# Expert stage of a transformer block: 32 by 32 turns on VectorE, two buffers for fetched rows, gate and up in four column tiles each

## The chip, the cores and the metric

One core of a Trainium2 chip runs the whole program. The metric is the device time of one execution in microseconds (us). The engines are TensorE (PE in the profile, with PEld for its weight loads), VectorE (DVE), ScalarE (ACT), GpSimd (POOL) and SyncE (SP), which issues most transfers. A profiled execution gives the trace that is read here.

## The reference, cut to what matters

The block attends and mixes (left out here), then sends each of 2048 tokens to two of 32 experts:

```
def hierarchical_moe(h, w_rg, w_re, w_g, w_u, w_d):
    ...
    eid = (group_idx[:, None] * EXPERTS_PER_GROUP + top_i.astype(jnp.int32)).reshape(-1)
    ...
    def expert_block(args):
        xb, e = args
        return (jax.nn.silu(xb @ w_g[e]) * (xb @ w_u[e])) @ w_d[e]
    ...
    y = jnp.sum(out[slot_dest].reshape(n_tok, TOP_K, D) * gates[..., None].astype(h.dtype), axis=1)
```

D_MODEL is 1024, D_EXPERT 512, everything is float32. An expert has three matrices of 2 MB each.

## The kernel before

The program runs in stages: projections, attention, time mixing, then the three stages that the change touches.

- `mix_out_and_route` (L1726): for each of 16 tiles of 128 tokens, the output projection, the second norm (h2, written to DRAM at L1781) and the router. `by_chunk` (L1720) reorders the channels within each row of h2, so that a block of 128 columns of h2 holds every fourth channel of a half. The router's weights w_r and the experts' weights are loaded in the same order (L1684, L1792, L1793).
- `place_slots` (L1984): the tables that say for each block of 32 rows which token rows to fetch (`from_all`), where to add the result (`to_all`) and the gate of each row (`gate_all`). Each of the 32 experts has at least two blocks of 32 rows; with these inputs there are 144 blocks.
- `run_experts` (L2132): the 144 blocks. All five engines run loops over the blocks and wait for each other by semaphores that count blocks.

In `run_experts` a block is 32 token rows. Every row is stored as four quarters of 256 channels on four partitions, so that a fetched block `xg` is 128 partitions by 256. POOL fetches it with an indirect DMA (`gather`, L2214), and adds a finished block to the output with another (L2225, 128 partitions by 256 as well). There is one buffer xg. TensorE turns xg with two 128 by 128 transposes (`turn`, L2249), ScalarE and VectorE copy one half each to xT. `gate_up` (L2255) works in four column tiles of 32: two take gate's halves of 256 columns, two take up's, all into one tile gu_ps, in 8 steps over the channels. ScalarE makes silu of the gate half, VectorE multiplies it with the row's gate and the up half to h (L2371). TensorE turns h by two transposes (`turn_h`, L2262), ScalarE copies it to hT, and `down` (L2270) multiplies it with wd in four column tiles of 256 columns and 4 steps. ScalarE and VectorE copy one half of y each (L2329, L2360).

TensorE's order in a block b (`one_block`, L2274) is: first half of gate_up(b), turn_h (block b-1), second half of gate_up(b), turn(b+1), down(b-1). Its code is a loop over three experts (L2305), and for each expert a first block and an inner loop over the others (L2289), so the loop over three experts holds six block bodies. POOL's order in a block (`one_block`, L2217) is: wait for the turn of xg, fetch, wait for y, add. VectorE's semaphore wait for the landing of an earlier add (`stored`) stands ahead of its copy of y. SP loads the weights of expert e+3 when expert e's last down is done (`refill`, L2195), twelve transfers of 512 KB.

A float32 matmul of the code stands in the trace as two MATMUL records, each with its LDWEIGHTS record; a transpose stands as one. So a block has 64 records of gate_up, 32 of down and 4 of transposes, and as many weight loads.

Of the kernel before, what the change touches and what calls it, by code (L numbers as in the profile page):

```python
# [20 lines left out]
ALU = mybir.AluOpType  # L21
# [1630 lines left out]
class ExpertWeights:  # L1652
# [20 lines left out]
    def load(self, sp, turn, s, part=None):  # L1673

        w_g, w_u, w_d = self.dram
        e = turn % N_GROUPS * PER_GROUP + turn // N_GROUPS
        for x, (to, src) in enumerate(((self.wg, w_g), (self.wu, w_u))):
            if part in (None, x):  # L1680
                rows = src[0, bass.ds(e, 1), :, :].rearrange("o (h p k) f -> p (o h) k f", h=2, p=P)
                for h in range(2):
                    for ks in (slice(0, 2), slice(2, 4)):
                        sp.dma_start(to[s][:, 4 * h + ks.start:4 * h + ks.stop, :], rows[:, h, ks, :]).then_inc(self.gu_loaded[s], 16)  # L1684
        if part in (None, 2):
            rows = w_d[0, bass.ds(e, 1), :, :].rearrange("o (f p) d -> p (o f) d", p=P)
            for f in range(FF // P):
                sp.dma_start(self.wd[s][:, f, :], rows[:, f, :]).then_inc(self.d_loaded[s], 16)
# [31 lines left out]
def by_chunk(row):  # L1720


    return row.rearrange("t (p k) -> t k p", p=P)


def mix_out_and_route(nc, program, E_all, ranks, gates, totals, x, norm2_gain, w_rg, w_re, experts, mix, ps, x1_dram, h2_dram):  # L1726


    with ExitStack() as ctx:
# [42 lines left out]
        with nc.Block() as block:  # L1772
            @block.sync
            def _(sp):
# [15 lines left out]
                for h in range(2):  # L1790
                    ks, rows = slice(4 * h, 4 * h + 4), slice(512 * h, 512 * h + 512)
                    sp.dma_start(w_r[:, ks, 0:N_GROUPS], w_rg[0, rows, :].rearrange("(p k) c -> p k c", p=P)).then_inc(weights, 16)  # L1792
                    sp.dma_start(w_r[:, ks, N_GROUPS:NL], w_re[0, rows, :].rearrange("(p k) c -> p k c", p=P)).then_inc(weights, 16)  # L1793
# [44 lines left out]
            def _(pe):  # L1838
# [13 lines left out]
                def one_tile(t, s, n, first, last):  # L1852
# [12 lines left out]
                    if first:  # L1865
                        pe.wait_ge(weights, 64)
# [37 lines left out]
            def _(dve):  # L1904
# [8 lines left out]
                def norm(t, s, n):  # L1913
# [9 lines left out]
                    for half in range(2):  # L1923
                        cols = slice(512 * half, 512 * half + 512)
                        done = dve.scalar_tensor_tensor(h2[:, s, cols].rearrange("t (k p) -> t k p", p=P), by_chunk(x_t[:, s, cols]), rstd[:, :],
                                                        by_chunk(gain[:, cols]), ALU.mult, ALU.mult)
# [57 lines left out]
def place_slots(nc, program, E_all, ranks, totals, gates, n_blocks, first_block, n_pairs, from_all, to_all, gate_all):  # L1984
# [5 lines left out]
    with ExitStack() as ctx:  # L1990
        sb, pb, sem = makers(nc, ctx, program)
        QUARTERS = [slice(q * ROWS, (q + 1) * ROWS) for q in range(4)]
        LO, HI = QUARTERS[0], slice(2 * ROWS, 4 * ROWS)
# [14 lines left out]
        spread = sb("spread", [ROWS, 4, ROWS])  # L2008
# [4 lines left out]
        token_ps, gate_ps, to_ps = pb("token_ps", [P, 512]), pb("gate_ps", [P, 512]), pb("to_ps", [P, 512])  # L2013
# [4 lines left out]
        with nc.Block() as block:  # L2018
            @block.gpsimd
            def _(pool):  # L2020
# [7 lines left out]
                pool.affine_select(out=spread[:, :, :], in_=spread[:, :, :], compare_op=ALU.not_equal, fill=1.0, base=0,  # L2028
                                   pattern=[[0, 4], [-1, ROWS]], channel_multiplier=1)
# [12 lines left out]
            def _(pe):  # L2042
                for part in range(PARTS):
                    pe.wait_ge(rows_ready, part * 2 + 2)
                    pe.wait_ge(gates_ready, part + 1)
                    for col in range(part * EACH, (part + 1) * EACH):
                        first, last = col == 0, col == 2 * NT - 1
                        pe.matmul(token_ps[LO, 0:TABLE], row_token[:, col, :], in_block[:, col, :], start=first, stop=last)
                        for q in (2, 3):
                            done = pe.matmul(gate_ps[QUARTERS[q], 0:TABLE], row_gate[:, col, :], in_block[:, col, :], start=first, stop=last)  # L2050
                done.then_inc(tabled, 1)
                pe.wait_ge(to_ready, 1)
                pe.matmul(to_ps[:, 0:TABLE], spread[:, :, :].rearrange("t q r -> t (q r)"), to_f[:, :], start=True, stop=True).then_inc(spread_done, 1)

            @block.vector
            def _(dve):
# [59 lines left out]
                dve.tensor_copy(gate_all[HI, :], gate_ps[HI, 0:TABLE])  # L2116
# [3 lines left out]
                dve.tensor_copy(to_row[:, :], to_ps[:, 0:TABLE])  # L2120
                dve.drain()
# [10 lines left out]
def run_experts(nc, program, n_blocks, first_block, n_pairs, from_all, to_all, gate_all, experts, h2_dram, out):  # L2132
# [6 lines left out]

    with ExitStack() as ctx:  # L2140
# [3 lines left out]
        LO, HI = slice(0, 2 * ROWS), slice(2 * ROWS, 4 * ROWS)  # L2144
# [5 lines left out]
        xg = sb("xg", [P, 2, P])  # L2150
        xT = sb("xT", [P, 2, 4, ROWS])
# [292 lines left out]
```

## Time and profile before

| | us |
|---|---|
| median of 3 runs | 3070.25 (3064.46 to 3083.59) |
| the profiled execution, its own time | 3088.86 |
| its span, first to last instruction | 3086.9 |
| the expert stage in it | about 2067 to 3080 |

Durations come from that one profiled execution. The mean granted clock of TensorE over its span is 0.973 of 2.4 GHz.

### The profile page before, as it was taken

What the parts mean: (1) busy time and instruction counts of PE and PEld (TensorE: products, weight loads), DVE (VectorE), ACT (ScalarE), POOL (GpSimd) and SP (SyncE); (2) the same over time, 40 slices, a digit from 0 to 9 for tenths busy, and PEclk for the clock granted to TensorE, in tenths of its full rate; (3) what the DMA queues carried; (4) which work ended last, traced back from release to release, by engine and by line L of the source; (5) the groups of instructions that cost most, each with busy time, mean ns of one, the idle gap of its engine ahead of it and who ended that gap; (6) DMA issues with size and microseconds to landing.
All of it is one profiled execution on the core that took longest, in us unless ns stands there. A gap on an engine that the chain in (4) does not pass through costs nothing. (4 is left out here: it accounts for less than half of the span.)

```text
span 3086.9 us, 87281 instructions
## 1 busy us (share of the span) xinstructions
PE 2812.0 (91%) x36552; PEld 1653.7 (54%) x36553; DVE 1277.1 (41%) x2547; ACT 975.2 (32%) x2057; POOL 808.5 (26%) x818
## 2 busy tenths in 40 slices
PE   8999999999999996888888899959888899898988
PEld 4444444444666665777777455534444444444444
DVE  2333221114887885667666244442222222222222
ACT  1211100003666665555554234311211112121211
POOL 0000300000110104666655000023333333333333
PEclk9999999999999998999999999969999999999999
DMA  3212131112022020111110255326777766777682
GB/s 127 68 51 68 46 112 54 61 61 91 8 69 66 10 91 22 38 42 43 39 52 25 70 204 203 116 103 201 236 236 239 236 218 208 260 242 253 202 280 42
DMA packets 208454, 370.01 MB, mean 120 GB/s; under 512 B 35057, under 2 KB 134897, under 8 KB 205554
## 3 DMA queue, kind: packets, MB, share of 16 engines
q1 hardware_dynamic: 180450, 328.72, 30.9%
q0 software_dynamic: 27792, 38.16, 6.3%
q8 instruction: 170, 2.79, 0.4%
q14 instruction: 42, 0.34, 0.0%
HBM read 296.30 MB, written 70.52 MB: 119 GB/s over the span
## 5 line engine op out<-in xcount | busy, mean ns | idle before, releaser
L2255 PE MATMUL gu_ps<-wg_,xT 128*32 128x256 f32 x3168 | 383.1, 384 | 7.0 <-issue 4.2
L2255 PE MATMUL gu_ps<-wu_,xT 128*32 128x256 f32 x3168 | 383.0, 384 | 0.0
L712 DVE TENSOR_TENSOR_SCAN h_all<-h_all 128x512 f32<-128x512 f32 (+3 forms) x320 | 345.8, 1130 | 69.0 <-ACT h_all L664 42.9
L344 PE MATMUL ps<-low,high 128*128 128x512 f32 x768 | 337.2, 596 | 2.4 <-issue 2.4
L2225 POOL DMA_INDIRECT out<-y,put x144 | 228.8, 1589 | 302.2 <-DVE y L2360 292.3
L2270 PE MATMUL y_ps<-wd_,hT 128*32 128x256 f32 x4608 | 297.2, 401 | 0.0
L2353 DVE COPY xT<-xT_ps 128x128 f32<-128x128 f32 x145 | 42.4, 292 | 534.7 <-PE xT_ps L2249 534.7
L2255 PEld LDWEIGHTS gu_ps<-wg_,xT 128*32 128x32 f32 x3168 | 180.4, 111 | 140.0 <-issue 22.3
L1714 PE MATMUL ps<-high 128*128 128x512 f32 x512 | 231.4, 602 | 8.5 <-DMA high<-mixT 8.1
L344 PEld LDWEIGHTS ps<-low,high 128*128 128x128 f32 x768 | 144.4, 191 | 173.0 <-issue 173.0
L2214 POOL DMA_INDIRECT xg<-h,take x147 | 145.7, 991 | 343.8 <-DVE take L2363 320.6
L690 POOL TENSOR_SCALAR_AFFINE_SELECT h_all<-h_all 128x256 f32<-128x256 f32 x64 | 39.8, 622 | 703.5 <-ACT h_all L664 703.3
L2270 PEld LDWEIGHTS y_ps<-wd_,hT 128*32 128x32 f32 x4608 | 140.6, 114 | 108.1 <-issue 39.4
L444 PE MATMUL ps<-h_all,w_first 128*128 128x512 f32 x448 | 193.6, 592 | 0.0
L664 ACT ACTIVATE h_all<-ps 128x1024 f32<-128x1024 f32 (+3 forms) x160 | 143.7, 899 | 151.6 <-PE ps L617 151.5
L2255 PE MATMUL gu_ps<-high,xT 128*32 128x256 f32 x2880 | 176.4, 386 | 0.0
L2255 PEld LDWEIGHTS gu_ps<-wu_,xT 128*32 128x32 f32 x3168 | 176.0, 111 | 0.0
L628 PEld LDWEIGHTS ps<-ident,h_all 128*128 128x128 f32 x1088 | 116.0, 141 | 106.9 <-DVE h_all L712 76.6
L444 PE MATMUL ps<-h_all,low 128*128 128x512 f32 x384 | 165.8, 592 | 0.0
L628 PE MATMUL ps<-ident,h_all 128*128 128x128 f32 x1088 | 154.8, 281 | 4.6 <-DVE h_all L712 4.1
L1714 PEld LDWEIGHTS ps<-high 128*128 128x128 f32 x512 | 95.1, 192 | 114.7 <-issue 114.0
L2249 PE MATMUL xT_ps<-ident,xg 128*128 128x128 f32 x292 | 64.1, 302 | 101.0 <-DMA xg<-h,take 101.0
(320 smaller groups left out, 4579.3 us busy)
## 6 DMA issues: line engine op xcount, KB each, us to landing
wd_<-in_w_exp_down SPq DMA_DIRECT2D x128, 512.0 KB
wg_<-in_w_exp_gate SPq DMA_DIRECT2D x88, 512.0 KB
wu_<-in_w_exp_up SPq DMA_DIRECT2D x88, 512.0 KB
high<-in_w_exp_gate SPq DMA_DIRECT2D x40, 512.0 KB
high<-in_w_exp_up SPq DMA_DIRECT2D x40, 512.0 KB
pT<-low SPq DMA_DIRECT2D x13, 1024.0 KB, 3.9
rkv<-pT SPq DMA_DIRECT2D x96, 128.0 KB, 2.5
high<-in_x SPq DMA_DIRECT2D x16, 512.0 KB, 4.0
```

Of the source, the lines that this page charges most:

```text
L344: done = pe.matmul(qkv_ps[:, part, :], hT[:, s, k, :], w_sb[:, k, part * SBW:(part + 1) * SBW], start=(k == 0), stop=(k == KT - 1))
L444: last = pe.matmul(p_ps[:, s, g, :], w[s][:, k, :], h_all[:, k, g * GT:(g + 1) * GT], start=(k == 0), stop=(k == KT - 1))
L628: last = pe.transpose(prodT_ps[h][:, b * P:(b + 1) * P], prod[:, n % KEPT, h, b * P:(b + 1) * P], ident[:, :])
L664: act.activation(keep[:, n % KEPT, :, 0:w], z_ps[n % 2][:, :, 0:w], ACT.Sigmoid, scale=-SCALE).then_inc(kept, 1)
L712: dve.tensor_tensor_scan(prod[:, n % KEPT, h, 0:w][:, ::-1], rows, rows, so_far, ALU.mult, ALU.bypass).then_inc(scanned, 1)
L1714: done = pe.matmul(self.ps[:, s, half, :], self.rows[:, s, k, :], self.w[:, k, half * 512:(half + 1) * 512], start=(k == 0), stop=(k == KT ...
L2214: pool.indirect_dma_start(out=xg[:, :, :].rearrange("t a b -> t (a b)"), out_offset=None, in_=h2_quarters[:, :], in_offset=bass.IndirectOf ...
L2225: pool.indirect_dma_start(out=out_quarters[:, :], out_offset=bass.IndirectOffsetOnAxis(ap=put[j][:, 0:1], axis=0), in_=y[j][:, :], in_offs ...
L2249: last = pe.transpose(xT_ps[j][:, 0:P], xg[:, j, :], ident[:, :])
L2255: last = pe.matmul(gu_ps[QUARTERS[q], 0:256], xT[:, k % 2, k // 2, :], w[s][:, k, half * 256:(half + 1) * 256], start=(k == 0), stop=(k == ...
L2270: last = pe.matmul(y_ps[QUARTERS[q], 0:256], hT[:, f % 2, f // 2, :], wd[s][:, f, q * 256:(q + 1) * 256], start=(f == 0), stop=(f == FT - 1))
L2353: dve.tensor_copy(xT[:, 1, :, :], xT_ps[1][:, 0:P].rearrange("p (q t) -> p q t", q=4)).then_inc(xT_ready, 1)
```

## The change

- The experts' turns move from TensorE to VectorE, whose transpose turns each 32 by 32 piece by itself (128 by 256 for the rows, 128 by 128 for h). The layouts of h2, of w_r and of the experts' weights are reordered to fit. The PSUM tiles of the turns, ident and both copies behind each turn are gone.
- xg becomes two buffers with a semaphore each. POOL fetches block b+4 into the buffer of b once h of block b+1 is done.
- Gate and up get a PSUM tile each and four column tiles of 128 columns each: 32 matmuls of the code for gate, then 32 for up, where there were 32 of 256 columns for both.
- sil, h and gate are 128 partitions wide instead of 64. ScalarE copies all of y alone. VectorE writes `put`, the row numbers for the add, at the end of its block, and waits for `stored` there.
- place_slots makes one copy of the gates and spreads it to four with one more matmul; w_r is loaded in 16 transfers instead of 4; the norm's last step is 4 instructions of 256 columns instead of 2 of 512.

```diff
-                rows = src[0, bass.ds(e, 1), :, :].rearrange("o (h p k) f -> p (o h) k f", h=2, p=P)
-                for h in range(2):
-                    for ks in (slice(0, 2), slice(2, 4)):
-                        sp.dma_start(to[s][:, 4 * h + ks.start:4 * h + ks.stop, :], rows[:, h, ks, :]).then_inc(self.gu_loaded[s], 16)
+                rows = src[0, bass.ds(e, 1), :, :].rearrange("o (p k) f -> p (o k) f", p=P)
+                for k in range(0, KT, 2):
+                    sp.dma_start(to[s][:, k:k + 2, :], rows[:, k:k + 2, :]).then_inc(self.gu_loaded[s], 16)
...
+                for j in range(4):
+                    for cols, src in ((slice(0, N_GROUPS), w_rg), (slice(N_GROUPS, NL), w_re)):
+                        rows = src[0].rearrange("(q p h j) c -> j h p q c", q=4, p=32, h=2, j=4)
+                        for h in range(2):
+                            sp.dma_start(w_r[32 * j:32 * j + 32, h::2, cols], rows[j, h]).then_inc(weights, 16)
...
-                def one_block(b, j, i, first):
-                    pool.wait_ge(turned, b + 3)
-                    pool.sem_inc(on_pool, 1)
-                    pool.wait_ge(rows_known, b + 4)
-                    pool.sem_inc(on_pool, 1)
-                    gather(1 - j)
-                    pool.wait_ge(y_copied, b * 2 + CREDIT + 2)
+                def add(b, j):
+                    pool.wait_ge(rows_known, b + 3)
                     pool.sem_inc(on_pool, 1)
+                    pool.wait_ge(y_copied, b + CREDIT + 1)
+                    pool.sem_inc(on_pool, 1)
                     pool.indirect_dma_start(out=out_quarters[:, :], out_offset=bass.IndirectOffsetOnAxis(ap=put[j][:, 0:1], axis=0),
                                             in_=y[j][:, :], in_offset=None, compute_op=ALU.add).then_inc(stored[j], 16)
+                def one_block(b, j, i, first):
+                    pool.wait_ge(h_ready, b + 3)
+                    pool.sem_inc(on_pool, 1)
+                    gather(j)
+                    add(b, j)
...
+                def project(to_ps, w, done):
+                    for k in range(KT):
+                        for q in range(4):
+                            last = pe.matmul(to_ps[QUARTERS[q], 0:P], xT[:, k * ROWS:(k + 1) * ROWS], w[:, k, q * P:(q + 1) * P],
                                              start=(k == 0), stop=(k == KT - 1))
+                    last.then_inc(done, 1)
+
+                def gate_up(b, s):
+                    pe.wait_ge(h_ready, b + 1)
+                    project(gate_ps, wg[s], gate_done)
+                    project(up_ps, wu[s], up_done)
...
                 def rest_of_expert(e, start, s):
                     with pe.Fori(1, count_of(pe, e)) as n:
-                        one_block(start + n, start + n - 1, s, s)
+                        gate_up(start + n, s)
+                        down(start + n - 1, s)
...
+                def turn_rows(j, i):
+                    dve.wait_ge(gathered[j], i * 16 + 16)
+                    dve.transpose(xT[:, :], xg[j][:, :])
+
+                def number_rows(b, j, i):
                     if not isinstance(i, int) or i > 0:
                         dve.wait_ge(stored[j], i * 16)
+                    dve.tensor_copy(put[j][:, :], to_all[:, bass.ds(b, 1)]).then_inc(rows_known, 1)
...
                 def one_block(b, j, i, first):
-                    dve.tensor_copy(gate[j][HI, :], gate_all[HI, bass.ds(b, 1)])
+                    dve.tensor_copy(gate[j][:, :], gate_all[:, bass.ds(b, 1)])
                     dve.drain()
-                    copy_xT(b + 1)
+                    dve.wait_ge(up_done, b + 1)
+                    turn_rows(1 - j, i + j)
                     next_rows(1 - j, b + 3)
                     dve.wait_ge(silu_ready, b + 1)
-                    dve.scalar_tensor_tensor(h[HI, :], sil[HI, :], gate[j][HI, :], gu_ps[HI, 0:256],
-                                             ALU.mult, ALU.mult).then_inc(h_ready, 1)
+                    dve.scalar_tensor_tensor(h[:, :], sil[:, :], gate[j][:, :], up_ps[:, 0:P], ALU.mult, ALU.mult).then_inc(h_ready, 1)
+                    dve.drain()
                     if not first:
-                        copy_y(b - 1, 1 - j, i - 1 + j)
+                        dve.wait_ge(y_done, b)
+                    dve.transpose(hT[:, :], h[:, :]).then_inc(hT_ready, 1)
+                    number_rows(b, j, i)
```

## Rows read from the trace of the kernel before

**Rows 1.** Busy time by stretch: busy us of each engine (records), clock, DMA.
```profile
1950.00:2000.00 50.00, 50.00 (x178) 26.89 (x177) 21.98 (x85) 20.40 (x30) 0.00 (x0) 1.00 0.30 111
2400.00:2600.00 200.00, 180.94 (x2845) 97.19 (x2838) 47.59 (x171) 39.24 (x128) 72.99 (x58) 0.97 0.70 220
1214.00:1708.00 494.00, 415.08 (x14597) 369.63 (x14598) 338.03 (x587) 254.08 (x517) 297.06 (x308) 0.99 0.14 39
```

**Rows 2.** Waits of the expert stage, then SP's own: us in total, times, longest.
```profile
PE xT_ps L2249 <- DMA xg<-h,take: 101.0, 47, 12.3
...
SPq L1684 <- PE y_ps L2270: 694.1, 29, 42.5
```

**Rows 3.** Chain of waits, pieces in the expert stage: start, us, what.
```profile
2112.10 7.14 DMA xg<-h,take
2149.03 5.56 DMA xg<-h,take
2356.69 8.29 DMA xg<-h,take
3070.35 2.77 DMA xg<-h,take
```

**Rows 4.** Timeline of TensorE in undisturbed blocks: start, us, records.
```profile
2079.86 0.44 PE L2249 MATMUL xT_ps<-ident,xg 128*128 128x128 f32 x2
2085.95 0.44 PE L2249 MATMUL xT_ps<-ident,xg 128*128 128x128 f32 x2
...
2403.55 0.39 PE L2255 MATMUL gu_ps<-wg_,xT 128*32 128x256 f32 x2
2403.77 0.39 PE L2255 MATMUL gu_ps<-wg_,xT 128*32 128x256 f32 x2
2405.39 0.33 PE L2262 MATMUL hT_ps<-ident,h 64*128 64x64 f32 x2
```

**Rows 5.** TensorE's first wait, a later one, and the clock behind it.
```profile
2067.18 0.66 PE L2249 MATMUL xT_ps<-ident,xg 128*128 128x128 f32 x2 [12.30 <-DMA xg<-h,take]
...
2119.38 0.66 PE L2249 MATMUL xT_ps<-ident,xg 128*128 128x128 f32 x2 [2.50 <-DMA xg<-h,take]
...
2119.40:2122.80 3.40, 3.40 (x30) 1.62 (x34) 0.93 (x3) 0.27 (x1) 0.99 (x1) 0.50 1.07 366
```

**Rows 6.** Timeline of TensorE in attention and in place_slots: column tiles side by side.
```profile
1101.35 1.09 PE L643 MATMUL ps<-h_all 128*64 128x128 f32 x16
...
2046.04 0.33 PE L2048 MATMUL token_ps<-in_block,row_token 128*32 128x196 f32 x1
2046.21 0.33 PE L2048 MATMUL token_ps<-in_block,row_token 128*32 128x196 f32 x1
```

**Rows 7.** Timeline of VectorE in one block.
```profile
2408.51 0.49 DVE L2371 SCALAR_TENSOR_TENSOR h<-sil,gate,gu_ps 64x256 f32<-64x256 f32 x1
2410.49 0.15 DVE L2359 COPY put<-to_all 128x1 int32 x1 [1.50 <-PE y_ps L2270]
2410.66 0.43 DVE L2360 COPY y<-y_ps 64x256 f32<-64x256 f32 x1
```

**Rows 8.** Groups of VectorE instructions of 128 by 256 from SBUF: busy us, mean ns.
```profile
L2095 DVE TENSOR_TENSOR row_token<-in_row,token 128x256 f32<-128x256 f32 x4 | 2.7, 681 | 0.3
L2090 DVE TENSOR_TENSOR in_row<-count,part_f 128x256 f32<-128x256 f32 x4 | 1.7, 415 | 0.1
```

**Rows 9.** Timeline of POOL in the same block: one fetch, one add.
```profile
2408.91 0.99 POOL L2214 DMA_INDIRECT xg<-h,take  x1 [1.50 <-DVE take L2363]
2411.93 1.59 POOL L2225 DMA_INDIRECT out<-y,put  x1 [2.03 <-DVE y L2360]
```

**Rows 10.** DMA queues, 1214 to 1708 us, then 2170 to 3035 us: packets, MB.
```profile
q8 instruction: 115, 1.88, 1.6%
...
q8 instruction: 1, 0.02, 0.0%
```

**Rows 11.** Timeline of SP ahead of the router's first tile.
```profile
1759.74 1.50 SPq L1792 DMA_DIRECT2D w_r<-in_w_router_group  x1
...
1767.17 2.04 SPq L1684 DMA_DIRECT2D wg_<-in_w_exp_gate  x4
```

More of the change, by code:

```diff
@@ L1922, in norm @@
                     dve.drain()
[L1923 to L1926, printed above, removed]
+                    for q in range(4):
+                        done = dve.scalar_tensor_tensor(h2[:, s, q * 256:(q + 1) * 256].rearrange("t (k p) -> t k p", k=KT), by_quarter(x_t[:, s, :], q),
+                                                        rstd[:, :], by_quarter(gain[:, :], q), ALU.mult, ALU.mult)
                     done.then_inc(h2_ready, 1)
@@ L2226, in one_block @@
                                             in_=y[j][:, :], in_offset=None, compute_op=ALU.add).then_inc(stored[j], 16)
[L2228 to L2239 removed]
+                def one_block(b, j, i, first):
[3 more added lines that the diff above has]
+                    add(b, j)
+                pool.wait_ge(rows_known, 2)
+                for j in range(2):
+                    gather(j)
+                for j in range(2):
+                    pool.wait_ge(h_ready, j + 1)
+                    gather(j)
+                last = last_pair(pool)
+                pairs_of_blocks(pool, last, one_block)
+                for j in range(2):
+                    add(last * 2 + j, j)
+                for j in range(2):
+                    pool.wait_ge(gathered[j], last * 16 + 32)
+                    pool.sem_inc(on_pool, 1)
+                    pool.wait_ge(stored[j], last * 16 + 16)
                     pool.sem_inc(on_pool, 1)
@@ L2244, in _ @@
             def _(pe):
-                def turn(b):
-                    pe.wait_ge(gathered, b * 16 + 16)
-                    pe.sem_inc(on_pe, 1)
-                    for j in range(2):
-                        last = pe.transpose(xT_ps[j][:, 0:P], xg[:, j, :], ident[:, :])
-                    last.then_inc(turned, 1)
-                def gate_up(b, s, ks):
-                    for k in ks:
-                        for q, (w, half) in enumerate(((wg, 0), (wg, 1), (wu, 0), (wu, 1))):
-                            last = pe.matmul(gu_ps[QUARTERS[q], 0:256], xT[:, k % 2, k // 2, :], w[s][:, k, half * 256:(half + 1) * 256],
-                                             start=(k == 0), stop=(k == KT - 1))
-                    if KT - 1 in ks:
-                        last.then_inc(gu_done, 1)
@@ L2272, in down @@
                     last.then_inc(y_done, 1)
-                def one_block(b, before, s, s_before):
-                    pe.wait_ge(xT_ready, b * 2 + 2)
-                    pe.wait_ge(h_ready, b)
-                    gate_up(b, s, range(0, KT // 2))
-                    turn_h()
-                    gate_up(b, s, range(KT // 2, KT))
-                    turn(b + 1)
-                    down(before, s_before)
                 def weights_of(s, n):
@@ L2294, in one_expert @@
                     weights_of(s, n)
-                    one_block(start, start - 1, s, (s - 1) % SLOTS)
+                    gate_up(start, s)
+                    down(start - 1, (s - 1) % SLOTS)
                     rest_of_expert(e, start, s)
-                pe.wait_ge(consts, 1)
-                turn(0)
                 weights_of(0, 0)
-                pe.wait_ge(xT_ready, 2)
-                gate_up(0, 0, range(0, KT))
-                turn(1)
+                gate_up(0, 0)
                 rest_of_expert(0, 0, 0)
```

140 lines of the change are left out of this document (46 added, 94 removed).

## The prediction, made before the changed kernel was run

> **What bounds the kernel now.** I read the busy times by stretch first, to see whether TensorE is the limit where the change works. It is busy for 50 of 50 us in the router's stage and for 181 of 200 in the expert stage, where VectorE has 48, ScalarE 39 and POOL 73; the weight transfers leave 3 tenths of the DMA engines free [rows 1]. The waits say what the missing tenth is: TensorE stood 101.0 us in 47 waits for a fetched block, 12.3 of them before the first block [rows 2, 5]. SP waited 694 us for slots to come free, in 29 waits, so the weights are early and bound nothing [rows 2]. The chain of waits shows the reason. A fetch takes 2.8 us from issue to landing with no weights under way and 5.5 to 8.3 beside them [rows 3], and with one buffer it can start only when TensorE has turned the block before, one block (6.09 us) ahead of its use.
>
> The timeline of TensorE in undisturbed blocks gives the unit. From one turn to the next are 6.09 us; four records of 256 columns, one on each column tile, start every 0.216 us [rows 4]. A block has 96 such records, 24 groups of four: 24 x 0.216 = 5.18. The other 0.91 are the two turns with the seams around them. So 144 blocks are 877 us; the fetch waits behind the first are 101.0 - 12.3 = 89; a stage of about 1013 leaves some 47. Of these, around 30 are the clock: at a mean granted clock of 0.97 [rows 1] the share at the lower level (1.2 of 2.4 GHz) is 0.06, which over 1010 us is 60 us at half speed. A row shows how one such stretch comes: a wait of 2.50 us for a fetch, and behind it 3.4 us at 0.50 [rows 5].
>
> **The parts of the change.**
>
> TensorE's block. The 64 records of 256 columns become 128 of 128. The nearest row for 128 rows by 128 columns is attention's: 16 records on two column tiles take 1.09 us; without the last one's own 0.27 that is 0.82 for the 7 steps between 8 pairs, 0.117 us each, the first step slower than the others [rows 6]. Half of 0.216 is 0.108. Three tiles of 196 columns start every 0.165 us [rows 6], so the time of a group goes with the columns of one tile (0.84 ns each in both), and not with the number of records: in time mixing 14597 of them ran in 494 us, 34 ns each with all its waits [rows 1], where 0.216 over four is 54. I take 0.109 for a group, 0.117 as the upper bound. Gate and up: 32 x 0.109 = 3.49; down: 8 x 0.216 = 1.73; seams 0.05. That is 5.27 instead of 6.09: 144 x 0.82 = **-118 us** (at 0.117: -81).
>
> VectorE between up and the next gate. TensorE may not start gate_up(b+1) before h(b), and VectorE turns the next rows ahead of h. The cover is down(b-1), 1.73 us. No row shows a transpose. The nearest instructions of 128 by 256 from SBUF take 0.42 and 0.68 us [rows 8]. With 0.15 for the row numbers, at most 0.49 for the product (64 by 256 today [rows 7]; 128 by 128 should be 0.36) and some 0.2 of handing over the sum is 1.1 to 1.5. It stays under the cover: nothing, and from a transpose of 0.9 us on each further 0.1 costs 14 us. hT has the whole of gate_up(b+1), 3.5 us, as cover. ScalarE's undivided copy of y has it too.
>
> The Trainium skill, VectorE: DVE Perf Modes, section The three transpose paths, gives 311 ns for 128 by 128 in bf16. An estimate from that page for twice the columns is some 0.45 us; no row here shows it, and the sum does without it.
>
> The fetches. The request for block b+4 goes out at h(b+1), and it is turned at the end of up(b+3): 2 x 5.27 - 1.4 = 9.1 us later, and the chain shows 8.3 at most [rows 3]. All 89 us of fetch waits go: **-89**. The order on POOL is fetch, then add. Between the last copy's end (2411.09) and the add's start are 0.84 us, and a fetch holds POOL for 0.99 and an add for 1.59 [rows 7, 9]; with both handovers that is 4.3 of 5.27 us, so POOL stays within a block.
>
> What is late next: the adds. VectorE's wait for `stored` moves to the end of its block, and block b waits there for the add of b-2 (before, for that of b-3 at about the same place). Behind it are queued the next gate copy, the turn of the next rows and h, and for h waits TensorE. Counted from the end of up(b): h(b) 1.3, down(b-1) over at 1.9, ScalarE's copy 0.4, POOL starts the add 0.84 later and a fetch may hold it up a little, so 3.5. Then the add's time L to its landing; then row numbers, gate, turn, product and handovers, 1.5; then gate_up(b+3), 3.5. Three blocks can't be shorter than 8.5 + L. At 3 x 5.27 = 15.8 an L of 7.3 costs nothing. No row gives L. The same bytes fetched take 2.8 alone and 5.5 to 8.3 beside weights, and an add issues 0.6 longer [rows 3, 9]: 3.4 alone, 6.1 to 8.9 beside weights. Each weight load queues twelve transfers at once just when the last down of an expert is done, so one add for each of the 29 loads meets the full queue: 8.9 - 7.3 and the handing over, 2 us, 58 in all, and some 7 from others: **+65**. Bounds: 0, if adds are as quick as fetches, and +125, if all beside the weights take 8.9 (a block of 5.8 for some 120 blocks, and the 58).
>
> The clock. Waits of over 2 us for fetches are gone, but the late adds leave a wait of the same length, and half of them. I take half of the 27 to 30 us: **-13** (0 to -27).
>
> TensorE's code. The loop over three experts holds six block bodies of 200 records today, about 1280 instructions with its branches; after, six of 320, about 2000. In time mixing 29195 records of TensorE ran with 115 packets of instructions, 254 to a packet; in the expert stage one packet came in 865 us [rows 1, 10]. So today's loop is held near the engine and straight code is fetched. Whether 2000 are held no row shows. If not, each of the 9 jumps back waits for at least one transfer, 2.8 us like an idle fetch, with a clock drop behind it (1.7): 40, up to 60 if more of the code comes late. Between 0 and 60 I take **+20**; the packet of today's loop is the only row, and it is silent on the longer one.
>
> The stages ahead. w_r's four loads held SP for 7.4 us (1759.74 to 1767.17 [rows 11]), and 16 with as many elements may hold it up to twice that, with TensorE waiting 1 us for them; place_slots has one more matrix product, one copy and one fill on its chain, about 1; the norm's four steps lie under TensorE's full load. The start of the expert stage loses two copies. **+2** (0 to +10).
>
> The sum: -118 - 89 + 65 - 13 + 20 + 2 = -133. Against the profiled execution: 3088.9 - 133 = 2956. That execution is 18.6 us above the median, which no step touches; the prediction is for the median, 3070.25 - 133 = **2937 us**.
>
> **The rivals.**
>
> 1. The records, not the columns, set TensorE's pace (slower than before). 0.216 over four is 54 ns and 0.165 over three is 55 ns: both rows would also fit a fixed price for each record. Gate and up would be 32 x 0.216 = 6.9, the block 8.7, +2.6 x 144 = +374, less 89 and 27: 3070 + 258 = 3328. It decides from 0.138 us for a group of 128 columns on: the other terms come to -15, and there the block is 0.10 longer than today's. Against it: 34 ns a record in time mixing [rows 1] and the pairs at 0.117 [rows 6]. Chance 0.05.
> 2. The adds take the fetches' place everywhere, L near 8.9 or more: -118 - 89 + 125 + 20 + 2 = -60, 3010. For it: an add reads and writes its rows, a fetch reads only. Chance 0.17.
> 3. The adds are in time and the code is held: -118 - 89 - 27 + 2 = -232, 2838. Chance 0.17.
> 4. The loop no longer stays near the engine and each lap pays for it in full, and the seams are wider: 60 instead of 20, and 0.117 a group: +77, 3014. The Trainium skill, Runtime: NRT & Kernel Launch, section Instruction fetch mechanics, says that TensorE holds 2048 instructions in blocks of 256 and that a taken branch to a block no longer held stalls; a loop of 2000 with a block fetched ahead would be over that. The trace agrees as far as it goes, with 254 a packet and none for today's loop. Chance 0.13.
> 5. The change doesn't do what it says: VectorE's transpose is far longer than the rows of its size, over 1.4 us, and TensorE waits for h instead of for xg: half a microsecond a block, +72, 3009. Chance 0.05.
>
> **How the numbers follow.** The forecast has 0.43: one late add an expert, the code between held and not, TensorE by columns. The range of 8 in 10 goes from rival 3 to just above rivals 2, 4 and 5: 2838 to 3035. Under 1 per cent (31 us) a measurement can't tell a change from none. All cases but the first lie more than that under 3070, though the upper three by only 56 to 61 us; I give 0.05 of them to within 1 per cent and 0.03 to slower, for bounds that prove too low. Faster by over 1 per cent 0.87, within 0.05, slower 0.08.
>
> **What the profile after would show.** TensorE's groups of gate and up start every 0.109 us, a block every 5.3. Waits of TensorE for xg are gone; VectorE waits for `up_done` at the turn, and in about one block in five its `put` waits for a transfer, with TensorE's wait for h behind it. VectorE's transposes are at 0.4 to 0.7 and 0.3 to 0.4 us. Packets of instructions in the expert stage stay at one or rise to some 80, with a wait at each third expert's start. The prediction is wrong if a group takes over 0.12 us, if adds beside weights take over 9 us, or if TensorE's wait for h stands in every block.

## The result, and the profile after

The changed kernel takes **3344.66 us** (3338.16 to 3353.67, 3 runs) against 3070.25: 1.0888 times as long, with a 95% interval of 1.0819 to 1.0957. Forecast were 2937 us and a range of 2838 to 3035. The profiled execution spans 3336.4 us at a mean granted clock of 0.917 (before: 3086.9 at 0.973).

The same views as before the change, first the busy times in the middle of the expert stage [rows 1], with two shorter stretches to which I come below. The columns are the same: busy us of each engine, clock, DMA share, GB/s.

```profile
2400.00:2600.00 200.00, 127.72 (x3576) 106.60 (x3572) 29.79 (x137) 16.26 (x56) 56.86 (x45) 0.82 0.63 191
...
2454.00:2458.00 4.00, 0.00 (x0) 0.00 (x0) 0.15 (x1) 0.00 (x0) 0.00 (x0) 0.50 0.94 315
2460.00:2478.00 18.00, 14.11 (x372) 12.25 (x376) 2.19 (x10) 1.45 (x5) 3.56 (x3) 0.76 0.40 136
```

TensorE is busy for 64% of this stretch instead of 90%, and its clock is 0.82. The transfers run at 191 GB/s instead of 220, at a DMA share of 0.63 instead of 0.70. The waits from 2060 us on, and SP's own, name what is missing [rows 2]:

```profile
DVE put L2323 <- DMA out<-y,put: 410.4, 110, 6.5
...
PE gate_ps L2246 <- DMA wd_<-in_w_exp_down: 365.6, 26, 21.3
```

```profile
SPq L1683 <- PE y_ps L2260: 29.8, 4, 25.6
```

SP, which had waited 694 us for free slots, now waits 30: it is never done with loading. TensorE waits for wd once in nearly every expert, 14 us on average. The chain that ended last, which was TensorE's and the fetches' before (21 and 10% of the span), is SP's. The two lines give its share of the whole span, of which the stage is 37%, by engine and by line; in the stretch from 2060 us on, SP's lines L1687 and L1683 have 37% each.

```profile
SPq 30%; DMA 3%; PE 2%; issue 1%; DVE 0%; POOL 0%; DVEq 0%; ACT 0%; POOLq 0%; ACTq 0%
SPq L1687 15%; SPq L1683 15%; DMA wd_<-in_w_exp_down 2%; PE gate_ps L2246 1%; PE up_ps L2246 1%; PE y_ps L2260 1%; SPq L2170 1%; DMA out<-y,put 0%; DMA xg<-h,take 0%; DVE xT L2318 0%; POOL out L2215 0%; DVE h L2332 0%; SPq L2198 0%; POOL xg L2207 0%; ACT y L2297 0%
```

SP's timeline shows two loads of an expert, each line the start and the time that SP spent on four transfers:

```profile
2399.77 11.53 SPq L1683 DMA_DIRECT2D wg_<-in_w_exp_gate  x4
2411.39 8.79 SPq L1683 DMA_DIRECT2D wu_<-in_w_exp_up  x4
2420.27 17.87 SPq L1687 DMA_DIRECT2D wd_<-in_w_exp_down  x4
2439.68 12.95 SPq L1683 DMA_DIRECT2D high<-in_w_exp_gate  x4
2452.73 5.67 SPq L1683 DMA_DIRECT2D high<-in_w_exp_up  x4
2458.49 20.49 SPq L1687 DMA_DIRECT2D wd_<-in_w_exp_down  x4
```

A load takes 39.9 us (2399.77 to 2439.68). From 2157.96 us on, 28 of them follow each other without a pause up to 3273.7, 1116 of the stage's 1224 us. SP's times aren't quite those of the transfers, as SP runs some transfers ahead of them: the DMA share falls some 3 us after SP's first transfer of wd and stays low some 5 us into the next wg. While wd goes, the DMA share falls from 0.94 to 0.40 and the rate from 315 to 136 GB/s (the stretches above), fetches and adds included. Where none of these is under way, the share is 0.26, about four of 16 engines:

```profile
2424.00:2427.00 3.00, 2.40 (x48) 2.30 (x52) 0.00 (x0) 0.00 (x0) 0.00 (x0) 0.50 0.26 107
```

By single microseconds the low stretch lasts from 2423 to 2445, so wd, a third of a load's bytes, takes some 22 of the 39.9 us. TensorE's own timeline, beside it, is as forecast:

```profile
2404.91 1.91 PE L2260 MATMUL y_ps<-wd_,hT 128*32 128x256 f32 x32
2424.60 3.42 PE L2246 MATMUL gate_ps<-wg_,xT 128*32 128x128 f32 x64 [17.78 <-DMA wd_<-in_w_exp_down]
2427.84 1.92 PE L2246 MATMUL up_ps<-wu_,xT 128*32 128x128 f32 x64
2429.59 1.90 PE L2260 MATMUL y_ps<-wd_,hT 128*32 128x256 f32 x32
2431.31 1.92 PE L2246 MATMUL gate_ps<-wg_,xT 128*32 128x128 f32 x64
2433.06 1.16 PE L2246 MATMUL up_ps<-wu_,xT 128*32 128x128 f32 x36
```

From up to up are 5.22 us. The gate products right behind the wait of 17.78 us take 3.24 instead of 1.75, at half clock. The groups of this kernel that answer to [rows 8] and to the mixing stage (busy us, mean ns, then idle time and what ended it):

```profile
L1713 PE MATMUL ps<-high 128*128 128x512 f32 x512 | 236.5, 613 | 34.1 <-DMA high<-mixT 33.9 <-issue 0.2
L2318 DVE STREAM_TRANSPOSE xT<-xg 128x256 f32<-128x256 f32 x145 | 64.6, 445 | 534.1 <-PE up_ps L2246 503.6 <-issue 23.0 <-DMA xg<-h,take 7.4
L2332 DVE SCALAR_TENSOR_TENSOR h<-sil,gate,up_ps 128x128 f32<-128x128 f32 x144 | 48.0, 334 | 0.0
L2336 DVE STREAM_TRANSPOSE hT<-h 128x128 f32<-128x128 f32 x144 | 44.9, 312 | 73.4 <-PE y_ps L2260 68.7
```

VectorE's transposes cost what the estimate said. The first row is a cost that I had not looked for: two experts' wd are loaded while the router works, and there they hold up SP's loads of mixT; TensorE waits 33.9 us for them, where it waited 8.1 before.

### The profile page after: what moved, and what is told of

It reads as the page before. It is cut to its first block and busy times, and to the rows that moved or that the text cites. A ratio compares the mean times of both kernels' runs of the same rounds, so it can differ in the third digit from the quotient of the medians.

```text
span 3336.4 us, 103696 instructions
## 1 busy us (share of the span) xinstructions
PE 2729.9 (82%) x45126; PEld 1859.5 (56%) x45127; DVE 1227.2 (37%) x2580; ACT 880.6 (26%) x1768; POOL 805.3 (24%) x815
## 3 DMA queue, kind: packets, MB, share of 16 engines
q1 hardware_dynamic: 179106, 328.72, 30.0%
## 5 line engine op out<-in xcount | busy, mean ns | idle before, releaser
L2246 PE MATMUL gate_ps<-wg_,xT 128*32 128x128 f32 x6336 | 223.7, 301 | 286.2 <-DMA wd_<-in_w_exp_down 268.8
L2246 PEld LDWEIGHTS gate_ps<-wg_,xT 128*32 128x32 f32 x6336 | 197.3, 122 | 321.2 <-issue 277.9
L2260 PE MATMUL y_ps<-wd_,hT 128*32 128x256 f32 x4608 | 274.4, 379 | 0.6 <-ACT y L2297 0.6
L1713 PE MATMUL ps<-high 128*128 128x512 f32 x512 | 236.5, 613 | 34.1 <-DMA high<-mixT 33.9
L2318 DVE STREAM_TRANSPOSE xT<-xg 128x256 f32<-128x256 f32 x145 | 64.6, 445 | 534.1 <-PE up_ps L2246 503.6
L2303 ACT ACTIVATE sil<-gate_ps 128x128 f32<-128x128 f32 x144 | 40.0, 278 | 644.4 <-PE gate_ps L2246 644.4
L2246 PE MATMUL gate_ps<-high,xT 128*32 128x128 f32 x2880 | 102.5, 303 | 124.1 <-DMA wd_<-in_w_exp_down 96.8
L2246 PE MATMUL up_ps<-wu_,xT 128*32 128x128 f32 x6336 | 200.4, 281 | 0.0
L2246 PEld LDWEIGHTS up_ps<-wu_,xT 128*32 128x32 f32 x6336 | 184.5, 115 | 1.5
L2297 ACT COPY y<-y_ps 128x256 f32<-128x256 f32 x144 | 53.7, 373 | 482.5 <-PE y_ps L2260 467.2
L2323 DVE COPY put<-to_all 128x1 int32 (+1 forms) x144 | 20.7, 144 | 410.4 <-DMA out<-y,put 410.4
```

The lines of the kernel that those rows point to most:

```text
L1713: done = pe.matmul(self.ps[:, s, half, :], self.rows[:, s, k, :], self.w[:, k, half * 512:(half + 1) * 512], start=(k == 0), stop=(k == KT ...
L2246: last = pe.matmul(to_ps[QUARTERS[q], 0:P], xT[:, k * ROWS:(k + 1) * ROWS], w[:, k, q * P:(q + 1) * P], start=(k == 0), stop=(k == KT - 1))
L2260: last = pe.matmul(y_ps[QUARTERS[q], 0:256], hT[:, k * ROWS:(k + 1) * ROWS], wd[s][:, k, q * 256:(q + 1) * 256], start=(k == 0), stop=(k = ...
```

## The experiments

Each ratio is against the kernel before, run on the same chip.

**First batch: is it wd?** In the change, `rows` of wd is `(o q) k p d` with q=4 and goes to 128 partitions in one transfer: the outermost dimension on the DRAM side counts four. `e1` gives each quarter of the partitions a transfer of its own, the same bytes to the same places:

```
-            rows = ....rearrange("o (q k p) d -> (o q) k p d", q=4, k=FF // P)
-            for k in range(FF // P):
-                sp.dma_start(self.wd[s][:, k, :], rows[:, k, :, :])
+            rows = ....rearrange("o (q k p) d -> (o q) p k d", q=4, k=FF // P)
+            for q in range(4):
+                sp.dma_start(self.wd[s][q * ROWS:(q + 1) * ROWS, :, :], rows[q, :, :, :])
```

> The changed kernel with one edit: the four transfers of an expert's down weights go by quarters of the partitions (32 partitions, 4 steps of 4 KB each) instead of by steps (4 groups of 32 partitions with one step); the bytes, the places and the number of transfers are the same. Theory A (a transfer whose outermost dimension is 4 runs on 4 of the 16 DMA engines, so the down weights take 18 us instead of 7 and TensorE waits for them 26 times, 366 us): those waits are gone, the time falls to what the forecast had, 2900 to 3000 us. Theory B (the weights are late because the code of the loop, the fetches and the adds crowd the DMA engines or SP's queue): the time stays within 3 per cent of 3345.

Measured: 3158.48 us, ratio 1.0204 (1.0181 to 1.0227), outside both expectations. TensorE's waits for wd are gone.

`e2` is the kernel before with the change's wd transfers put in and nothing else (the products with wd then pair other rows, so the output is another).

> The kernel before with only the changed kernel's four transfers of the down weights (the rows then don't fit the order of hT, so the output is another). Theory A: each expert's weights take some 38 us instead of 20 and TensorE waits for them; about 30 experts x 38 to 40 us of transfers is over the stage's 1013 us, so 3250 to 3350 us. Theory B: 3070.

Measured: 3350.91 us in one run, where the kernel before took 3096.37. This edit alone makes the old kernel 8.2% slower, where the whole change makes it 8.9% slower. SP's timeline and TensorE's waits for wd from 2060 us on (its waits for fetches grow as well, from 101.0 to 164.7 us):

```profile
2421.38 19.81 SPq L1688 DMA_DIRECT2D wd_<-in_w_exp_down  x4
```

```profile
PE gu_ps L2255 <- DMA wd_<-in_w_exp_down: 100.8, 14, 16.3
```

`e3` is the changed kernel with the old, plain wd transfers (output another again, for the same reason).

> The changed kernel with the plain transfers of the kernel before for the down weights (128 partitions outermost; the rows then don't fit the order of hT, so the output is another). Theory A: as with transfers by quarters, within 1 per cent of it. If transfers over 32 partitions are slower than those over 128, this one is the faster of the two by more than 1 per cent. Theory B: 3345.

Measured: 3127.45 us in one run, 1.0% under `e1` by the ratios, at the edge of what the expectation asked for. The three runs say the same: the outermost count of four is what makes wd late. The Trainium skill has the rule in DMA: Bandwidth & Descriptors, section Why a DMA increments its semaphore by 16 and not by 1: a transfer is split over the largest number of engines, 16 at most, that divides the slowest dimension of both sides. That makes four here. The trace agrees: the DMA share is 0.26, and 2.10 MB in some 22 us are 95 GB/s. Before the change all engines were busy during a load, at 352 GB/s, of which a quarter is 88:

```profile
2484.00:2500.00 16.00, 13.22 (x220) 6.97 (x212) 3.33 (x12) 3.13 (x10) 5.98 (x5) 1.00 1.03 352
```

The count of packets fits too. The weights' queue of the changed kernel has 1536 packets fewer than that of `e1` and `e3` (180642, below), all of them under 512 bytes, and `e2` has 1536 fewer than the kernel before. That is 12 for each of wd's 128 transfers, what one small packet from each of 4 engines instead of 16 would give.

```profile
q1 hardware_dynamic: 179106, 328.72, 30.0%
```

But 3127 and 3158 are still above the kernel before, where I expected 4% below it. `e1`'s block lasts 6.9 to 7.0 us, and TensorE's timeline shows holes inside it:

```profile
2406.17 1.27 PE L2246 MATMUL gate_ps<-wg_,xT 128*32 128x128 f32 x40
2407.66 0.28 PE L2246 MATMUL gate_ps<-wg_,xT 128*32 128x128 f32 x1 [0.22 <-issue]
2408.35 0.42 PE L2246 MATMUL gate_ps<-wg_,xT 128*32 128x128 f32 x3 [0.42 <-issue]
2409.08 0.76 PE L2246 MATMUL gate_ps<-wg_,xT 128*32 128x128 f32 x18 [0.31 <-issue]
```

Forty records go at full pace, then for 1.8 us only four start: "issue" means that no semaphore holds them. The whole stage has 319 such waits of gate's products, 143.0 us with the longer stops at the laps (longest 8.2). Holes of this kind stand in some 77 of the 87 blocks between 2200 and 2850 us, in `e3` in some 80 of 89, and in the changed kernel in none. From here on I had two theories. S (supply): TensorE isn't fed with short records fast enough. Rivals: the columns alone set the time and something else in the change brings the holes (C), or the wait on the adds does (W).

**Second batch.** `e4`, the kernel before with 128-column products:

```
-                            last = pe.matmul(gu_ps[QUARTERS[q], 0:256], xT[...], w[s][:, k, half * 256:(half + 1) * 256], ...)
+                            last = pe.matmul(gu_ps[QUARTERS[q], c, 0:P], xT[...], w[s][:, k, half * 256 + c * P:half * 256 + (c + 1) * P], ...)
```

> The kernel before, with each product of gate and up over 256 columns made as two over 128 (into two banks of PSUM; the fetched rows are loaded as the standing operand twice as often). Same columns, same bytes, same engines; only TensorE's number of instructions grows, to that of the changed kernel and a little above. Theory S (supply): TensorE can't be fed short records steadily after a jump back or a stop, so the block of 6.09 us grows by the 1.5 to 2 us of issue gaps seen in the version that loads wd by quarters, and each round of the three-expert loop stops for about 8 us more: 3250 to 3400 us. Theory C (columns alone set the time, the gaps come from VectorE's turning, from the two fetch buffers or from the adds): within 1% of before, 3065 to 3125 us on this chip.

Measured: 3144.95 us, ratio 1.0262 (1.0242 to 1.0283). Between the two: short records cost 80 us by themselves, but the block has no holes. 265 packets of instructions were fetched instead of 170, and TensorE stopped 11 times ahead of gate's products, 38.3 us in all and 6.3 at most, once in each lap of the three-expert loop.

`e5`, `e1` with 256-column products:

```
+                        for q, (w, half) in enumerate(((wg, 0), (wg, 1), (wu, 0), (wu, 1))):
+                            last = pe.matmul(gate_ps[QUARTERS[q], 0:256], xT[...], w[s][:, k, half * 256:(half + 1) * 256], ...)
```

> The changed kernel with wd loaded by quarters, and gate and up made as 32 products of 256 columns in one tile in place of 64 of 128 in two (the pairing of gate and up columns is then another, so the output is another; work, bytes and the rest are the same; the silu starts only when up is done too). Theory S: half of the gate and up records take the gaps away, the block falls from 6.9 to 7.0 us to 5.3 to 5.6 and the rounds of the loop lose their long stops: 2900 to 3000 us. Theory C: the gaps stay where they are, 3130 to 3190 us.

Measured: 3034.56 us, ratio 0.9902 (0.9882 to 0.9922): 3% under `e1` and between the two expectations. The holes are gone, but VectorE's `put` waits for adds rose to 398.9 us, and TensorE waits 124.9 us for h behind them.

`e6`, `e1` with `number_rows` one block later:

```
                     dve.transpose(hT[:, :], h[:, :]).then_inc(hT_ready, 1)
-                    number_rows(b, j, i)
+                    if not first:
+                        number_rows(b - 1, 1 - j, i - 1 + j)
```

> The changed kernel with wd loaded by quarters, and the row numbers of an add written one block later on VectorE, so that its wait for the add before has a block more of time. Theory S: the adds have slack behind TensorE's gaps, 3140 to 3165 us. Rival (the wait on the adds holds VectorE and so the next block; 324 us of VectorE's idle time are put down to it): 3060 to 3130 us.

Measured: 3026.67 us, ratio 0.9876 (0.9856 to 0.9896). Below what either theory gave: the edit touches only VectorE's order, and TensorE's holes are gone too. VectorE's waits from 2060 us on, against 324.2 us in `e1`:

```profile
DVE put L2323 <- DMA out<-y,put: 45.4, 35, 3.0
```

`e7`, a mix: two fetch buffers and rows turned by VectorE as in the change; 256-column products, TensorE's own turning of h and plain wd as before; row numbers later.

> A mix: fetched rows in two buffers and turned by VectorE as in the change, but gate and up as products of 256 columns in one tile, the gated products turned by TensorE and copied by ScalarE as before, wd loaded as before, and the row numbers of an add written one block later. Theory S: TensorE loses its two transposes of rows and the waits on the fetch, has fewer instructions than before, and has no gaps; block 5.5 to 5.7 us, 2880 to 2960 us. Theory C: the turning or the two buffers bring the gaps along, 3060 to 3150 us.

Measured: **2903.3 us**, ratio 0.9469 (0.9453 to 0.9485). Busy times from 2200 to 2750 us: TensorE never stops and its clock is full.

```profile
2200.00:2750.00 550.00, 546.75 (x9550) 311.42 (x9542) 124.58 (x490) 108.82 (x341) 249.95 (x194) 1.00 0.87 293
```

That lies within theory S's range. So VectorE's turning of the rows and the two buffers together are good; no run has one without the other. What remained were the holes, the adds, and how wd should be loaded.

**Third batch.** `e9` and `e10` are `e1` with eight instructions that do nothing, at the start of VectorE's part of the stage or of TensorE's (`for _ in range(8): dve.drain()`, and `pe.drain()`).

> The changed kernel with wd loaded by quarters, and eight instructions that do nothing at the start of VectorE's part of the expert stage; the work is the same. In the version without them TensorE hardly issues for some 1.6 us beside each add that GpSimd issues, in the changed kernel itself and in the version with later row numbers it does not. Theory P (where the engines' code lies in memory decides that): the gaps may go, and with them up to 120 us: 3030 to 3100 us. Theory W (the wait on the add in VectorE's order brings the gaps): the same time, 3140 to 3170 us.

> The same with the eight instructions on TensorE, ahead of its first block, so that all code of its expert loop lies eight instructions further on. Theory P: the gaps beside the adds go or move, anything from 3030 to 3170 us, but not the same trace. Theory W: the same time and the same gaps, 3140 to 3170 us.

Measured: 3099.4 and 3108.51 us in one run each, the kernel before at 3065.61: 1.011 and 1.014 instead of 1.020. In both traces no block between 2200 and 2850 us has the holes. TensorE's timeline in `e9`, and POOL's; the add at 2416.84 is issued while TensorE runs at full pace, where in `e1` the add at 2407.70 lay exactly over the holes, although both come 1.5 us after the start of gate's products:

```profile
2415.30 1.93 PE L2246 MATMUL gate_ps<-wg_,xT 128*32 128x128 f32 x64
2417.05 1.93 PE L2246 MATMUL up_ps<-wu_,xT 128*32 128x128 f32 x64
2418.79 1.91 PE L2260 MATMUL y_ps<-wd_,hT 128*32 128x256 f32 x32
```

```profile
2416.84 1.59 POOL L2215 DMA_INDIRECT out<-y,put  x1 [0.38 <-issue]
```

```profile
2407.70 1.59 POOL L2215 DMA_INDIRECT out<-y,put  x1 [0.39 <-issue]
```

That refutes theory W, as VectorE's early wait stands in both, and speaks for P. It doesn't show P: the changed kernel and `e3` have the same 103696 instructions and differ in the access patterns of SP's four wd transfers alone, and yet only `e3` has the holes. Where the code lay in memory no run recorded.

As the source of the holes, short records (S) are refuted too: `e9`, `e10` and `e6` have them and no holes.

In place of the holes stands the next wait: `put` now waits 441.1 us for adds instead of 324.2, so that only 29 us are gained; that rests on one run of `e9`, and the kernel before varied by 14 us beside it. As neutral edits take the holes away, what `e5` and `e6` gained over `e1` can't be put down to their edits alone. The step from `e9` to `e6` is then about the price of VectorE's early wait for `stored` without the holes: 1.011 to 0.9876, 72 us. TensorE's waits for h, 106.6 us in 51 in `e9`, shrink to 0.9 in `e6`, and its stops at the laps grow.

`e8`: wg and wu of a slot in one tile, so that one product takes 128 columns of gate and 128 of up; otherwise `e6`.

```
+            both = sb(f"wgu{s}_", [P, 2, KT, FF])
+                            last = pe.matmul(gate_ps[QUARTERS[q], 0:256], xT[:, k * ROWS:(k + 1) * ROWS],
+                                             experts.w_gu[s][:, :, k, q * P:(q + 1) * P], start=(k == 0), stop=(k == KT - 1))
```

> The changed kernel with wd loaded by quarters, the row numbers of an add written one block later, and the weights of gate and up in one tile, so that each product takes 128 columns of gate and 128 of up at once: 32 products of 256 columns a block, the right pairing, all rows and gated products turned by VectorE. Theory S+W (the short records cost supply stops, and the wait on the add holds VectorE; both are taken away here): block 5.25 to 5.4 us against 5.65 in the mix that left the turning of h to TensorE, 2840 to 2890 us. If the adds and fetches themselves set the pace now (they land 7 to 9 us after their issue beside the weights), the block stays at 5.6 to 6 us: 2900 to 2960 us.

Measured: 2945.28 us, ratio 0.9613 (0.9539 to 0.9688), the second of the two outcomes. Busy times of the middle of the stage, and ScalarE's longest wait:

```profile
2400.00:2600.00 200.00, 179.97 (x3246) 104.06 (x3240) 44.36 (x202) 23.16 (x84) 87.51 (x69) 0.98 1.04 275
```

```profile
ACT y L2294 <- DMA out<-y,put: 354.4, 100, 8.3
```

The DMA engines are full (1.04) at 275 GB/s, and the adds behind the weights are late even with a block more of time. In `e7` they moved 293 GB/s at 0.87: the quarters are a poorer way to load wd than plain transfers. The page's line for the weights' queue shows it on two kernels that differ in how wd is loaded and in nothing else, `e1` and `e3` (packets, MB, share of 16 engines' span):

```profile
q1 hardware_dynamic: 180642, 328.72, 33.8%
```

```profile
q1 hardware_dynamic: 180642, 328.72, 30.1%
```

The same packets and bytes take 1064 us of the engines in one and 941 in the other. The Trainium skill, SBUF — State Buffer, section Door 1: The DMA port swizzle, says that 32 partitions next to each other reach 8 of the 16 ports by which transfers enter, and so half the rate. The direction agrees with the two lines; the ports themselves no run here shows.

**Fourth batch.** `e11` is `e8` with plain wd transfers, which fit as each product takes its columns in pieces of 32: then partition 32q+a of hT belongs to row 32q+a of a plain wd step.

```
+                        cols = experts.w_gu[s][:, :, k, :].rearrange("p g (j q a) -> p g j q a", q=4, a=ROWS)
+                            last = pe.matmul(gate_ps[QUARTERS[q], 0:256], xT[...], cols[:, :, :, q, :], ...)
```

> The version with gate and up in one tile and later row numbers, with one thing more: each product takes its 256 columns in pieces of 32 (column 32j+a of quarter q is column 128j+32q+a of the weights), so that wd needs no order of its own and is loaded as before, by four plain transfers of 128 partitions. If the loading by quarters held the fetches and adds back there (DMA share 1.04 at 275 GB/s against 0.87 at 292 in the mix with plain transfers), blocks fall from 6.07 to 5.3 to 5.5 us: 2830 to 2880 us. If it is the shorter block that leaves the adds no time, 2920 to 2950 us as with quarters. If pieces of 32 columns read slower than whole rows, TensorE's groups are longer than 0.216 us.

Measured: **2844.73 us**, ratio **0.9290** (0.9274 to 0.9305), the fastest of all: 99 us less than `e8`, from which it differs in wd's transfers and the order of the columns. Busy times, TensorE's timeline and ScalarE's wait for adds:

```profile
2400.00:2600.00 200.00, 198.80 (x3668) 122.53 (x3664) 46.97 (x229) 27.45 (x96) 98.00 (x77) 1.00 0.91 304
```

```profile
2410.72 3.64 PE L2249 MATMUL gate_ps<-high,xT 128*32 128x256 f32 x64
2414.17 1.92 PE L2258 MATMUL y_ps<-wd_,hT 128*32 128x256 f32 x32
2415.90 3.64 PE L2249 MATMUL gate_ps<-high,xT 128*32 128x256 f32 x64
```

```profile
ACT y L2295 <- DMA out<-y,put: 3.5, 2, 2.0
```

A block is 5.18 us, and columns in pieces of 32 cost nothing.

`e12` is the same with 64 products of 128 columns in two tiles, as in the change: the change itself, with wd plain, its columns in pieces of 32 and the row numbers later.

> The same plain loading of wd and later row numbers, but gate and up made as in the change, by 64 products of 128 columns in two tiles: against the version before it, the price of short products alone. Supply stops once in a round of the three-expert loop (8 to 9 us each, 10 or 11 rounds, and half clock behind them) make it 90 to 150 us slower than that version: 2930 to 3020 us. Without such a price it is within 1% of it.

Measured: 2938.36 us, ratio 0.9593 (0.9570 to 0.9615). The difference of 94 us is the price of short products, with the two tiles that they fill. TensorE's waits on issue make up some 63 of it (66.8 us against 3.5); half clock behind the stops is most of the rest. TensorE's timeline at the start of a lap, the clock behind it, and the page's line for instruction packets, here and in `e11`:

```profile
2416.85 1.91 PE L2261 MATMUL y_ps<-wd_,hT 128*32 128x256 f32 x32
2424.95 3.64 PE L2247 MATMUL gate_ps<-wg_,xT 128*32 128x128 f32 x64 [6.19 <-issue]
```

```profile
2424.90:2429.00 4.10, 4.05 (x77) 3.77 (x81) 0.00 (x0) 0.28 (x1) 0.00 (x0) 0.50 0.11 22
```

```profile
q8 instruction: 255, 4.18, 0.6%
```

```profile
q8 instruction: 169, 2.77, 0.4%
```

## Why the prediction was wrong, step by step

**The failed step** is "SP waited 694 us for slots to come free, in 29 waits, so the weights are early and bound nothing". It was true of the kernel before and I carried it over, though the change rewrites wd's own transfers (the lines are at `e1`); the sum has no term for wd. The runs showed weights that are hardly ever early: SP waits 29.8 us instead of 694, a load takes 39.9 us, and TensorE waits 365.6 us for wd in 26 waits. The missing term is the largest. From the change (1.0888) to `e9` (1.011), which differ in how wd is loaded and in eight instructions that do nothing, are 239 us; from `e6` (0.9876) to `e12` (0.9593), which load the same wd by quarters and plainly, another 87 (from `e8` to `e11` it is 99). About 25 of the 239 lie ahead of the stage: the waits for mixT are 33.9 us, where `e9` has 9.5, and TensorE's first product of the stage starts at 2101.2 us, in `e9` at 2076.0. With the rule cited above it could have been worked out from the trace of before: a quarter of 352 GB/s is 88, wd's 2.10 MB take 24 us at that, the other 4.2 MB 12 at 352, together 36 us an expert, where an expert's 4.5 blocks give 24.

**TensorE's block** was right: 5.22 us measured for 5.27, groups of 128 columns at 0.109. Rival 1, whose 3328 us is nearest to the result, is refuted all the same; the figure agrees by accident.

**VectorE under the cover of down** was right: 445 and 312 ns for the transposes, 334 for the product. **The fetch waits** did go. The wait for `xg` is VectorE's now, one of 7.4 us in the changed kernel and one of 7.3 in `e11`; only where the DMA engines are full do they come back (61.9 us in 43 waits in `e8`).

**The late adds**: +65 forecast, 72 measured from `e9` to `e6`, so the size came out right for a wrong reason. The order of the waits is as described, but neither their count nor L. In `e9` `put` waits 104 times and TensorE 51 times, instead of once in an expert. From the start of an add's issue to the end of the `put` wait that hangs on it are 7.3 to 10.0 us in the changed kernel (60 adds between 2200 and 2850 us, median 8.0) and 9.1 in the median of `e9`, 38 of 74 above 9: beyond the 8.9 of the sum, which the prediction had named as a sign of being wrong. In the changed kernel itself TensorE waits only 10.0 us for h, since it stands waiting for wd anyway. One block more of time took the waits away only where wd came plainly (3.5 us of ScalarE's waits in `e11`, 354.4 in `e8`).

**TensorE's code**: +20 forecast, up to 60; 94 measured. The mechanism was right, with 85 packets more where I had written "some 80", and a stop in each lap. What I mis-sized is the stop: not one transfer of 2.8 us, but 3.8 to 6.6 us in `e12` and half clock behind it. With `e4` the same edit cost 80. In the changed kernel the stops lie under the waits for wd, so what they cost there can't be read from it. Rival 4 had this mechanism. The Trainium skill, Runtime: NRT & Kernel Launch, section Instruction fetch mechanics, gives TensorE room for 2048 instructions, fetched 256 at a time. The trace agrees as far as a loop of about 1280 instructions is held (8 packets from 2060 us on, before and in `e11`) and one of about 2000 isn't (94 in `e12`).

**The clock**: -13 forecast. It went to 0.82 in the changed kernel's stage, as each wait for wd has half clock behind it; in `e11` it is 0.99 over the stage and 1.00 in its middle, near the forecast's far bound of -27.

**The stages ahead**: +2 forecast. TensorE's first product of the stage started at 2068.3 us before; it starts at 2066.6 in `e1` and between 2073 and 2076 in `e6`, `e9`, `e11` and `e12`, so from 1.7 us earlier to 7.7 later, where the bounds were 0 and +10. w_r's transfers hold SP for 9.4 us instead of 7.4.

With the two repairs (`e12`) the change has a ratio of 0.9593, or 2945 us against 3070.25, 8 from the forecast. That is partly chance: there the adds cost nothing where 65 were forecast, and the code 94 instead of 20. `e11`, where the adds are in time and the code is held, has 0.9290, or 2852 us; rival 3, which says just that, had 2838.

**Open**: why TensorE starves beside GpSimd's adds in some of these kernels and not in others. `e1` and `e3` have the holes in nearly all blocks, the change, `e6`, `e9`, `e10` and `e12` in none. Two neutral edits each took them away; the mechanism wasn't found, and where code lies is a guess. What the holes cost wasn't measured apart either: 29 us is what is left when the next wait takes their place.

## What to carry to other kernels

A diff that rearranges a transfer changes its speed, even if bytes, count and packet sizes stay: look at the outermost dimension on both sides and at how many partitions it fills, and ask of a queue that is "early" by how much it may slow down before it binds. If a layout is needed by one engine, let the engine whose access patterns are free take it (here TensorE's moving columns), and leave the transfer 128 partitions wide. Halving products in a loop doubles its instructions; if it then no longer stays held, every lap pays a stop (3.8 to 6.6 us here) and a stretch at half clock.

## What the hardware did that I had not expected

- A transfer of 0.52 MB to 128 partitions, whose DRAM side has an outermost dimension of four, takes about 5.5 us (22 over four; at 352 GB/s it would be 1.5), and the DMA share is 0.26 meanwhile if nothing else is under way.
- The same 328.72 MB in the same 180642 packets take 33.8% of the engines' span of 3149 us with wd by 32 partitions, 30.1% of 3126 with 128.
- TensorE reads moving columns in pieces of 32 as fast as whole rows: groups of four 256-column records every 0.216 us in both.
- Eight instructions that do nothing removed holes of 1.8 us a block; in one run each the kernel got 0.9 and 0.6 per cent faster, hardly more than such runs vary.
- An add of 128 by 256 beside weights takes 7.3 to 10.0 us from its issue to the wait's end in the changed kernel, where a fetch of the same bytes took 5.5 to 8.3 before.
